# A second feed-forward block by seven block products (Strassen) in place of eight, in a two-block kernel on one core

## The reference, cut to what matters

```
x = x + (gate_a * y_a + gate_b * y_b) @ w_out[i]
h = rmsnorm_2(x, g_ffn[i])
x = x + jnp.square(jax.nn.relu(h @ w_ffn_up[i])) @ w_ffn_down[i]
ple_gate = jax.nn.sigmoid(rmsnorm_2(x, g_ple[i]) @ w_ple_gate[i])
```

## Time and profile before

| | |
|---|---|
| median of 3 runs | 2951.04 us (2950.37 to 2951.27) |
| the profiled execution | span 2949.8 us from first to last instruction |
| PE busy | 2834.9 us, 96% of the span |
| DVE, ACT, POOL busy | 47%, 26%, 13% |
| DMA engines | 80 GB/s on the mean |

### The profile page before, as it was taken

The page is one execution under the profiler, slowest core; times in us unless marked ns, Lnnn a source line. Parts: engine busy times, 40 slices in busy tenths (PEclk is TensorE's granted clock), DMA queues, the critical chain, the costliest instruction groups (busy, mean ns, idle before and its releaser), DMA issues.

```text
span 2949.8 us, 37202 instructions
## 1 busy us (share of the span) xinstructions
PE 2834.9 (96%) x15872; PEld 2299.4 (78%) x15872; DVE 1383.5 (47%) x1890; ACT 758.3 (26%) x1027; POOL 378.6 (13%) x346
## 2 busy tenths in 40 slices
PE   6889999999999999999999899899999999999998
PEld 5677878888888888877777677678888888888876
DVE  6985443232332445545545666644433333334454
ACT  4143312111120331124444343322311111111232
POOL 2000111000010101000002502203211111101221
PEclk8899999999999999999999999989999999999999
DMA  4051011111111113335558034243111111111111
GB/s 179 23 129 64 29 62 53 43 58 43 44 57 43 58 32 124 123 134 151 157 159 220 15 88 154 91 150 121 55 46 43 57 43 47 53 43 57 44 57 58
DMA packets 222339, 236.87 MB, mean 80 GB/s; under 512 B 60160, under 2 KB 174720, under 8 KB 221280
## 3 DMA queue, kind: packets, MB, share of 16 engines
q1 hardware_dynamic: 222176, 234.49, 24.9%
HBM read 178.50 MB, written 56.20 MB: 80 GB/s over the span
## 4 chain that ended last, share of the span: by engine, by line
PE 86%; DVE 8%; ACT 3%; issue 2%; DMA 1%; POOL 1%; SPq 0%; DVEq 0%; ACTq 0%; POOLq 0%
PE bank L631 21%; PE bank L632 21%; PE bank L633 21%; PE bank L1839 2%; PE bank L1840 2%; PE bank L1841 2%; PE bank L2542 2%; PE bank L3308 1%; PE bank L3310 1%; PE bank L3309 1%; PE bank L2572 1%; PE bank L2799 1%; PE bank L3317 1%; DVE stat L2670 1%; DVE w_lo L183 1%
## 5 line engine op out<-in xcount | busy, mean ns | idle before, releaser
L631 PE MATMUL bank<-op_hi,w_hi 128*128 128x512 f32 x1824 | 712.5, 391 | 1.6 <-DVE gates L673 1.5
L632 PE MATMUL bank<-op_lo,w_hi 128*128 128x512 f32 x1824 | 710.6, 390 | 0.0
L633 PE MATMUL bank<-op_hi,w_lo 128*128 128x512 f32 x1824 | 710.6, 390 | 0.0
L631 PEld LDWEIGHTS bank<-op_hi,w_hi 128*128 128x128 f32 x1824 | 343.1, 188 | 73.4 <-issue 2.2
L633 PEld LDWEIGHTS bank<-op_hi,w_lo 128*128 128x128 f32 x1824 | 342.9, 188 | 71.8
L632 PEld LDWEIGHTS bank<-op_lo,w_hi 128*128 128x128 f32 x1824 | 343.0, 188 | 71.0 <-issue 0.2
L183 DVE TENSOR_TENSOR w_lo<-w_raw,w_hi 128x2048 fp32r<-128x2048 f32 (+3 forms) x119 | 256.6, 2156 | 191.2 <-ACT w_hi L433 187.0
L631 PE MATMUL bank<-f_hi,w_hi 128*128 128x512 f32 x864 | 337.0, 390 | 3.2 <-POOL f_lo L183 3.2
L632 PE MATMUL bank<-f_lo,w_hi 128*128 128x512 f32 x864 | 336.7, 390 | 0.0
L633 PE MATMUL bank<-f_hi,w_lo 128*128 128x512 f32 x864 | 336.6, 390 | 0.0
L183 DVE TENSOR_TENSOR hT<-hT,bank 128x512 f32<-128x512 f32 x256 | 169.8, 686 | 315.2 <-PE bank L633 314.8
(11 more groups left out here) (471 smaller groups left out, 3810.3 us busy)
## 6 DMA issues: line engine op xcount, KB each, us to landing
record<-record_scratch SPq DMA_DIRECT2D x16, 1024.0 KB, 5.4
w_raw<-in_w_ffn_up SPq DMA_DIRECT2D x16, 1024.0 KB, 5.1
w_raw<-in_w_ffn_down SPq DMA_DIRECT2D x16, 1024.0 KB, 4.9
...
```

The costliest lines, as they stand in the source:

```text
L631: t.matmul(ps[:], hi[:, k, wc], x[0][:, k, xc], start=n == 0, stop=False)
L632: t.matmul(ps[:], hi[:, k, wc], x[1][:, (k + turn) % KD, xc], start=False, stop=False)
L633: last = t.matmul(ps[:], lo[:, k, wc], x[0][:, k, xc], start=False, stop=n == kt - 1)
```

## The change

The product of two matrices cut into 2x2 blocks is made of seven block products in place of eight. The blocks here are: an output pair of 128-channel tiles, two halves of 512 tokens, and pairs of inner tiles. For a pair q (16 of up2, 24 of down2) the order of products is 0 to 4, product 0 of the next pair, 5 and 6 (`sevenfold`). Each product has 3 x depth matmuls into one bank, depth being half of the number of inner tiles: 4 in up2, and 2, 3, 3, 3, 3, 2 in the six chunks of down2, each of four pairs.

Some operands are sums of blocks. `Sevens.add` makes three sums and replaces one block, in four dependent steps: those of weights on POOL, those of the moving operands on DVE. `split_hi` (ACT) and `split_lo` (DVE, two inputs on chip, written in place) then make seven hi and seven lo operands. Three of up2's bank states and two of down2's are copied away by ACT ("kept", "kept d") before the bank goes on, and later added by DVE (up2) or POOL (down2).

up2 now runs as a whole before down2. Its results go to memory (f_scratch) and come back as the moving operands of down2's chunks; the residual hT2 goes out to h_scratch (`h2_dram`) and comes back too, since its place is used. The multiplication by rs is now partly POOL's. The waits that tie the engines in down2 are those of `ffn2_tensor`: product 2 waits for DVE's acc of product 0, 4 and 5 for the kept copies of 2 and 4, 6 for DVE's acc of product 3; each product waits for its own lo operands.

```diff
+    def add(self, e, i, step, js=slice(None), part=0):
+
+        a, c, b, d = (self.quarter(i, row, col, js) for col in range(2) for row in range(2))
+        q0, q1, q2 = (self.sums(i, n, js) for n in range(3))
+        if step:
+            e.wait_ge(*self.summed(i, part, step - 1))
+        if self.moving:
+            out, x, y, o = ((q1, d, b, ALU.subtract), (b, b, a, ALU.subtract), (q0, d, b, ALU.subtract),
+                            (q2, c, q0, ALU.subtract))[step]
+        else:
+            out, x, y, o = ((q1, a, b, ALU.subtract), (b, b, d, ALU.add), (q0, b, a, ALU.subtract),
+                            (q2, c, q0, ALU.subtract))[step]
+        tt(e, out, x, y, o).then_inc(*self.adder.up(self.name, "sum", i, part, step))
+
+    def summed(self, i, part=0, step=3):
+        return self.adder.of(self.name, "sum", i, part, step)
+
+    def split(self, i, n, part=0):
+        return self.V.of(self.name, "lo", i, n, part)
+
+    def add_all(self, e, i):
+        for step in range(4):
+            self.add(e, i, step)
+
+    def split_hi(self, s, i, n, js=slice(None), part=0, after=3):
+        s.wait_ge(*self.summed(i, part, after))
+        s.activation(self.hi(i, n, js), self.part(i, n, js), ACT.Copy).then_inc(
+            *self.A.up(self.name, "hi", i, n, part))
+
+    def split_lo(self, v, i, n, js=slice(None), part=0, after=3):
+        v.wait_ge(*self.summed(i, part, after))
+        v.wait_ge(*self.A.of(self.name, "hi", i, n, part))
+        tt(v, self.part(i, n, js, 1), self.part(i, n, js), self.hi(i, n, js), ALU.subtract).then_inc(
+            *self.V.up(self.name, "lo", i, n, part))
+
...
+def sevenfold(pairs):
+
+    for q in range(pairs):
+        if q == 0:
+            yield 0, 0
+        for n in range(1, 5):
+            yield q, n
+        if q + 1 < pairs:
+            yield q + 1, 0
+        yield q, 5
+        yield q, 6
+
+
+BANK_OF = "xyxzxxz"
...
+    def seven_products(t, T, name, q, n, w, x, i, parts=()):
+
+
+
+        bank = (name, BANK_OF[n], q)
+        ps = tile_of(t, "all", *bank) if n in (0, 1, 3) else psum.tile(*bank)
+        t.wait_ge(*w.split(q, n))
+        for part, js in enumerate(parts or (slice(None),)):
+            if parts:
+                t.wait_ge(*x.split(i, n, part))
+            for j in range(*js.indices(w.depths[q])):
+                start, end, more = j == 0 and n in (0, 1, 3), j == w.depths[q] - 1, n in (2, 4, 5, 6)
+                t.matmul(ps[:], w.hi(q, n)[:, j, :], x.hi(i, n)[:, j, :], start=start, stop=False, skip_group_check=more)
+                t.matmul(ps[:], w.hi(q, n)[:, j, :], x.part(i, n, lo=1)[:, j, :], start=False, stop=False,
+                         skip_group_check=more)
+                last = t.matmul(ps[:], w.part(q, n, lo=1)[:, j, :], x.hi(i, n)[:, j, :], start=False, stop=end,
+                                skip_group_check=more)
+        last.then_inc(*T.up(name, q, n))
 
     def halves_of(tiles, name):
 
@@ -1427,6 +1561,7 @@
...
+        for n in (0, 1, 6, 3, 4):
+            if n > 1:
+                s.wait_ge(*Sy.T.of("op", 5))
+            xu.split_hi(s, 0, n, EARLY)
+        for k in (6, 7):
+            scaled(k)
+        xu.split_hi(s, 0, 0, LATE, 1, 1)
+        s.wait_ge(*wt3.used(3))
+        for n, js, part in ((1, LATE, 1), (2, EARLY, 0), (2, LATE, 1), (3, LATE, 1)):
+            xu.split_hi(s, 0, n, js, part)
+        for k in (6, 7):
+            nm_f.square(s, k, hT2[:, k, :])
+        for n, js, part in ((4, LATE, 1), (5, EARLY, 0), (5, LATE, 1), (6, LATE, 1)):
+            xu.split_hi(s, 0, n, js, part)
         yield
...
+        for step in range(4):
+            v.wait_ge(*T.of("op", (1, 1, 3, 5)[step]))
+            xu.add(v, 0, step, EARLY)
+        for n in (0, 1, 6, 3, 4):
+            if n == 3:
                 yield from residual(6)
                 yield from residual(7)
-            v.wait_ge(*A.of("norm hi", k))
-            stt(v, op2[1][:, k, :], hT2[:, k, :], vec["g_ffn_2"][:, k:k + 1], op2[0][:, k, :], ALU.mult,
-                ALU.subtract).then_inc(*V.up("norm lo", k))
-        columns_vector(v, V, T, "cols y", ncol[:, 0, :])
-        v.wait_ge(*A.of("root"))
-        v.reciprocal(ncol[:, 0, :], ncol[:, 0, :]).then_inc(*V.up("rs_col"))
-        spread_vector(v, V, T, "rs y", mem.rs_b)
+            xu.split_lo(v, 0, n, EARLY)
+        v.wait_ge(*A.of("scaled", 7))
+        for step in range(4):
+            xu.add(v, 0, step, LATE, 1)
+            if step == 1:
+                xu.split_lo(v, 0, 0, LATE, 1, 1)
+        for n, js, part in ((1, LATE, 1), (2, EARLY, 0), (2, LATE, 1), (3, LATE, 1), (4, LATE, 1),
+                            (5, EARLY, 0), (5, LATE, 1), (6, LATE, 1)):
+            xu.split_lo(v, 0, n, js, part)
         yield
...
+    down_chunks = ((0, 2), (4, 3), (10, 3), (16, 3), (22, 3), (28, 2))
+    DOWN_PAIRS = 4 * len(down_chunks)
+    wd = Sevens("w_down", False, mem.w_dn, [h for _, h in down_chunks for _ in range(4)], d_seven, S2.G, S2.A, S2.V)
+    xf = Sevens("x_first", True, mem.x_first, (2,), d_moving, S2.V, S2.A, S2.V)
+    xd = Sevens("x_down", True, mem.x_down, [h for _, h in down_chunks[1:]], d_moving[::-1], S2.V, S2.A, S2.V)
...
+            seven_products(t, T, "down2", q, n, wd, x, i, (slice(None),) if q % 4 == 0 else ())
...
+            if k:
+                q0, n0 = down_order[k - 1]
+                if q0 < LAST_DOWN:
+                    wd.split_lo(v, q0 + 1, n0)
+                if q0 % 4 == 3 and q0 < LAST_DOWN:
+                    x, i = moving(q0 // 4 + 1)
+                    x.split_lo(v, i, n0)
+            if q % 4 == 2 and 1 <= n <= 4 and q // 4 + 1 < len(down_chunks):
+                x, i = moving(q // 4 + 1)
+                x.landed(v, i)
+                x.add(v, i, n - 1)
```

More of the change, by code:

```diff
@@ L239, in weights_at, with sevens, both @@
                 [self.put("w_lo", [P, n], F32R, o) for _, o in offsets])
+    def sevens(self, width, depth, hi, blocks):
+        def both(slot, name, shape):
+            return self.at(slot, name, shape), self.at(slot, name + "_lo", shape, F32R)
+        return ([self.at(s, "hi", [P, depth, width], F32R) for s in hi],
+                [(both(s, "block", [P, 2 * depth, 2, width]), [both(q, "sum", [P, depth, width]) for q in sums])
+                 for s, sums in blocks])
     def lay_out(self):
@@ L388, with __init__ @@
 class Weights:
-    def __init__(self, nc, name, tiles, plan, before=()):
+    def __init__(self, nc, name, tiles, plan, before=(), stage=None):
         self.name, self.plan, self.before = name, plan, before
@@ L3278, in ple_sync @@
     def ple_sync(q):
-        q.wait_ge(*S2.T.of("down2", last2, KD - 1, 1))
+        q.wait_ge(*S2.T.of("down2", LAST_DOWN, 6))
+        q.wait_ge(*S2.G.of("acc", LAST_DOWN, 4))
         q.dma_start(mem.pT[:], a["l_pT"].rearrange("(k p) t -> p k t", p=P)).then_inc(*d_ple_in.up(by=16))
```

523 lines of the change are left out of this document (384 added, 139 removed).

## The result

The changed kernel takes 2964.2 us (median of 4 runs, 2962.8 to 2965.8), the kernel before, beside it, 2951.2 (4 runs). The ratio is 1.0047, 95% interval 1.0035 to 1.0059: slower by half a per cent. Run again later, beside other kernels, it took 2961.4 (6 runs), ratio 1.0033 (1.0021 to 1.0045). The forecast was 2957, in a range of 2927 to 2977, with "slower" the likeliest.

A forecast was written before the change was run, and what follows sets the result against it. PE was taken to bound the kernel, a line of matmuls without a hole. The terms -87.1 + 27 + 20 + 36 + 7 + 3 = +5.9 us took the profiled 2949.8 to 2955.7, median 2957 us; range 2927 to 2977.

The forecast's parts named there:

- What is removed, -87.1: In up2 and down2 together, 384 fewer matmuls at 0.2267 us each: 87.1 us less.
- The rival in which the waits of each product cost 0.05 us: At each product's start, three waits cost PE 0.05 us each over 280 products: +14 us, 2971 us; chance 0.05.
- Start, +27: Start of ffn2: operand preparation delays products 0 and 2, 25 us lost, plus 1.8 us for the norm's sums.
- I was to be wrong if the start cost under 20: Sign against the prediction: at the start of ffn2, a cost below 20 us where +27 was forecast.
- up2 itself, 0: Within up2, DVE, ACT and POOL fit beside a pair's 19.05 us of PE, so nothing is lost: 0 us.
- The rival in which GpSimd and DVE lag there: In up2, POOL and DVE lag by one us a pair: +16 us, 2973 us; chance 0.18.
- From up2 to down2, +20: Between up2 and down2, PE waits: 0.7 for kept 4, 13.5 before product 2, 5 for kept 2 of pair 1.
- Changes of chunk, +36: At down2's five chunk changes, DVE's work plus POOL's hindrance exceeds PE's time: 13, three times 7, and 2 us.
- the sums hide: At down2's chunk changes, POOL seldom meets DVE, so they cost 5 to 10 us, not 36: 2929 us; chance 0.27.
- The share of hindrance, 0.7 of 14.7 us a change: At down2's chunk changes, POOL closes 14.7 us to DVE's two-input ops; 0.7 of that counts, 10.3 us.
- End, +7: From down2's last pair into `ple`: product 5's wait, POOL's squares and late first lo and norm sum cost 7 us.
- Clock, +3: After long PE waits, at the start and the two behind up2, half clock costs 1 us each.

## Why the prediction was right, and where it was off

- **What is removed, -87.1: right.** PE's starts are 0.2267 us apart at full clock in L772, L773 and L775, as between L632 and L633. The rival in which the waits of each product cost 0.05 us is refuted by the 1237 starts in 280 us of either kernel.
- **Start, +27: the chain right, the sum in part by luck**, 28.0. Product 2 was to start at 2138.7 and did at 2138.53. I had placed the wait of the first part at 8 us; it is 6.0, for I let PE end with the start of DVE's adds at 2108.30, and its last matmul ends at 2110.98 (2117.00 less 6.02), 0.75 of it since the whole stage is that much later here. So PE lost some 22 us up to product 2 (17.6 of waits, 4 of half speed) and not 25; what makes it up is 4.6 us of half speed in product 2 and behind the sums over columns, which the term did not have. I was to be wrong if the start cost under 20: in waits alone it did, with the half speed not.
- **up2 itself, 0: right.** The rival in which GpSimd and DVE lag there is refuted: no wait in 280 us.
- **From up2 to down2, +20: the waits right, 18.9**, and by their causes: 0.7, 2.8 and 10.4 for the forecast's 0.7 and 13.5, and 5.00 for kept 2 behind GpSimd's sums, forecast +5 (ACT stands 10.4 us for those sums, which follow the third block's landing). The half speed behind them, 7.8, was not in it.
- **Changes of chunk, +36: the mechanism right, the size a little off.** Waits of 9.6 us (forecast 13), then 3.0, 3.0 and 4.4 (7 each), and 2.35 (2): 22.3, with half speed 31.1. By length, against 30.6, 38.8 and 34.0 us of matmuls at the first, the middle three and the last, 13.0, 5.3, 3.8, 5.3 and 2.7 are lost, for 13, 7, 7, 7 and 2. DVE is the limit there, as forecast. What was too long is its list without hindrance, 35.6 us in the forecast and 33 to 34 at depth 3 (43.7 less 9.9, 42.2 less 9.1, 43.8 less 10.7): in the trace an instruction starts some 0.08 us before the recorded end of the one ahead, and I had added up recorded lengths. The rival *the sums hide* needed less than 24 in all; in waits alone it is met, with the half speed not, and its reason is refuted: GpSimd meets DVE at every change.
- **The share of hindrance, 0.7 of 14.7 us a change: right.** The table gives 11.6, 9.9, 9.1, 10.7 and 9.6 us, 10.2 on the mean, for the forecast's 10.3. The price was right for a sum of 128x384 (0.82 us more on an instruction of 128x1536, where I took 0.8) and a little low for an `hT` add (1.10, where I took 1.0). That the product comes out within 0.1 us is luck: both 0.8 and 0.7 were rough. The Trainium skill, page "SBUF — State Buffer", section "Who interferes with whom", says that a DVE instruction with two SBUF inputs and a GpSimd one that reads SBUF shut each other out for the whole instruction. The runs agree in that the bank-fed adds are untouched (0.68), the others stretched by most of the time that they lie beside a GpSimd instruction (2.84 for 1.75 where the two overlap for 1.23), and GpSimd's fills hinder nothing; the 13 us more that I had worked out from it are not there, since the whole is 51 us at the five changes and would have been 64.
- **End, +7: the waits 9.1**, with half speed 12.3; the longest, 4.35 for the first `op_lo`, was in it. The squares were not a cause.
- **Clock, +3: the step that failed.** I took 1 us each for three places. There are ten groups of 9 to 23 slow matmuls and twenty single ones, 28.4 us on PE. The reason that I gave, that what half speed costs lies mostly in the next wait, holds where a wait follows: at the start for 19 of 43, at the hand-over for the 14 behind the longest wait, and, which the runs do not show one by one, at the changes of chunk for most. Filling the waits gave 0.8 us in the first stretch, and in the later part 1.9 by the stretch or 3.5 by the medians for 6 us of half speed. The cost of its own is then some 11 to 15 us (an estimate: 24 matmuls at the start, 4.8, and a third to a half of what the later stages show, 20), and the rest hid waits that would have been there anyway; part of what the changes of chunk were cheaper by in waits is this. How it parts between the two at each wait was not settled.

The sum came out as +13.0 in the first set of runs and +9.8 in the last, against +5.9. Part of that nearness is luck: the waits and the sums over columns are 69.7 us where the other terms had 90, and half speed is 28.4 where its term had 3. The two errors nearly cancel; some 13 to 17 us of them are one thing under two names (half speed that hides a wait), the rest is chance.
